# One fp32r trunk of two layers on one core: residual, second products and outputs moved from feature-major to token-major

## The reference, cut to what matters

```python
for i in range(DEPTH):                       # DEPTH = 2
    sh_m, sc_m, gt_m, sh_f, sc_f, gt_f = split(silu(c) @ ada_w[i] + ada_b[i], 6)
    h = rms_norm(x, norm_g[i, 0]) * (1.0 + sc_m) + sh_m
    y = pool_mixer(h, pool_w, pool_scale) if i == 0 else short_conv_mixer(h, conv_in_w, conv_w, conv_out_w)
    x = x + gt_m * rms_norm(y, norm_g[i, 1])
    hf = rms_norm(x, norm_g[i, 2]) * (1.0 + sc_f) + sh_f
    x = x + gt_f * rms_norm(square(relu(hf @ w1[i])) @ w2[i], norm_g[i, 3])
```

## Time and profile before

| what | value |
|---|---|
| median of three runs | 1056.64 us |
| span of the profiled execution | 1051.8 us (no other time is listed for that execution) |
| TensorE busy | 1017.9 us, 97% |
| VectorE busy | 587.5 us, 56% |
| ScalarE busy | 376.3 us, 36% |
| GpSimd busy | 43.6 us, 4% |
| mean granted TensorE clock | 0.975 |
| DMA | 140.02 MB, mean 133 GB/s |

### The profile page before, as it was taken

One profiled execution on the slowest core, in us unless ns is written; L12 is line 12 of the kernel. 1 busy time (PEld: TensorE's weight loads), 2 busy tenths in 40 slices (PEclk: granted clock), 3 DMA queues, 4 the chain that ended last, 5 costly groups with the idle time before them and its releaser, 6 DMA issues.

```text
span 1051.8 us, 11746 instructions
## 1 busy us (share of the span) xinstructions
PE 1017.9 (97%) x4594; PEld 827.0 (79%) x4594; DVE 587.5 (56%) x666; ACT 376.3 (36%) x441; POOL 43.6 (4%) x54
## 2 busy tenths in 40 slices
PE   5879899999999999998999999999999999999998
PEld 5534688888888888887888888878888888888887
DVE  4685867547547637888544444685324433432644
ACT  5364443223115223373432325355114222411533
POOL 4001410000000000001000000110000000000000
PEclk9899799999999999998999999799999999999999
DMA  7966165544555555620323223113232322223212
GB/s 264 319 213 208 41 231 205 176 166 174 208 179 180 192 187 199 221 81 1 120 81 120 80 96 104 41 46 115 87 113 80 119 80 99 100 81 118 80 40 81
DMA packets 63349, 140.02 MB, mean 133 GB/s; under 512 B 3212, under 2 KB 12628, under 8 KB 63316
## 3 DMA queue, kind: packets, MB, share of 16 engines
q1 hardware_dynamic: 55252, 110.21, 31.5%
q10 hardware_dynamic: 8064, 29.36, 7.6%
HBM read 137.47 MB, written 2.10 MB: 133 GB/s over the span
## 4 chain that ended last, share of the span: by engine, by line
PE 90%; DVE 5%; DMA 4%; ACT 1%; issue 0%; SPq 0%; DVEq 0%
PE ps L362 27%; PE ps L363 27%; PE ps L364 27%; PE ps L431 2%; DMA raw<-in_ada_w_dram 2%; PE ps L422 2%; PE ps L398 1%; DMA ada_raw<-in_ada_w_dram 1%; DVE in_lo L921 1%; DVE ada_sum L819 1%; DMA raw<-in_x_dram 1%; DVE y L932 1%; DVE xs L926 1%; DVE y L917 1%; DVE xx_t L898 1%; PE ps L415 1%
## 5 line engine op out<-in xcount | busy, mean ns | idle before, releaser
L811 DVE TENSOR_TENSOR w_lo<-raw,w_hi 128x2048 fp32r<-128x2048 f32 x77 | 176.5, 2292 | 288.0 <-ACT w_hi L604 288.0
L604 ACT ACTIVATE w_hi<-raw 128x2048 fp32r<-128x2048 f32 x81 | 154.9, 1913 | 437.7 <-PE ps L364 408.8
L362 PE MATMUL ps<-in_hi,w_hi 128*128 128x512 f32 x704 | 275.2, 391 | 7.7 <-DVE in_lo L921 6.2
L363 PE MATMUL ps<-in_lo,w_hi 128*128 128x512 f32 x704 | 274.6, 390 | 0.0
L364 PE MATMUL ps<-in_hi,w_lo 128*128 128x512 f32 x704 | 274.4, 390 | 0.0
L362 PE MATMUL ps<-mid_hi,w_hi 128*128 128x512 f32 x576 | 224.2, 389 | 0.0
L364 PE MATMUL ps<-mid_hi,w_lo 128*128 128x512 f32 x576 | 224.1, 389 | 0.0
L363 PE MATMUL ps<-mid_lo,w_hi 128*128 128x512 f32 x576 | 224.1, 389 | 0.0
L362 PEld LDWEIGHTS ps<-in_hi,w_hi 128*128 128x128 f32 x704 | 132.6, 188 | 36.7 <-issue 4.8
L364 PEld LDWEIGHTS ps<-in_hi,w_lo 128*128 128x128 f32 x704 | 132.6, 188 | 27.6
L363 PEld LDWEIGHTS ps<-in_lo,w_hi 128*128 128x128 f32 x704 | 132.6, 188 | 27.4
(11 more groups left out here) (123 smaller groups left out, 659.5 us busy)
## 6 DMA issues: line engine op xcount, KB each, us to landing
raw<-in_ffn_w_dram SPq DMA_DIRECT2D x64, 1024.0 KB, 5.3
ada_raw<-in_ada_w_dram ACTq DMA_DIRECT2D x56, 512.0 KB, 5.6
ada_raw<-in_ada_w_dram SPq DMA_DIRECT2D x28, 512.0 KB, 5.2
raw<-in_conv_in_w_dram SPq DMA_DIRECT2D x16, 512.0 KB, 4.3
raw<-in_ada_w_dram SPq DMA_DIRECT2D x10, 512.0 KB, 6.8
raw<-in_conv_in_w_dram SPq DMA_DIRECT2D x4, 1024.0 KB, 5.1
raw<-in_conv_out_w_dram SPq DMA_DIRECT2D x4, 1024.0 KB, 5.0
raw<-in_x_dram SPq DMA_DIRECT2D x4, 512.0 KB, 5.2
```

What stands on the lines that cost most here:

```text
L362: nc.tensor.matmul(o, a, hi[:, chunks[kk], :], start=first and kk == 0, stop=False)
L363: nc.tensor.matmul(o, a, lo[:, chunks[kk], :], start=False, stop=False)
L604: nc.scalar.activation(w_hi[:, u % 2, :], raw[:, u % 2, :], ACT.Copy).then_inc(w_hi_ready, 1)
L811: nc.vector.tensor_tensor(w_lo[:, u % 2, :], raw[:, u % 2, :], w_hi[:, u % 2, :].bitcast(F32), ALU.subtract).then_inc(w_lo_ready, 1)
```

## The change

- xs and y hold 128 tokens on the partitions and 1024 channels along them (four token tiles). The second product of each MLP, the convolution's output product and the pool's product take the activations (mid_hi, mid_lo, in_hi, in_lo) as stationary operand and 512 (pool: 256) columns of weights as moving one, so that their output is token-major. First products stay as they were.
- The mean square is a ScalarE Square with accumulation along a tile, one root and one reciprocal per partition. Diagonals, sums over partitions by ones and `keep_warm` are gone.
- A boundary goes by token tile: y is finished, x made, scaled by a row (128 copies of 1+scale times g), shifted by a row, turned by eight transposes into two PSUM banks, rounded by ScalarE, and the low part made by VectorE. The last pair of units goes tile by tile and the first pair of the next sub-layer in two halves of 256 tokens.
- The gate, scale and shift rows of the first sub-layers are spread by TensorE (`spread_row`, `shift_unit`), the seven later ones by GpSimd (a sum over all partitions), which also fetches the norm weights, spreads them, clears the sums and loads biases into them.
- Split weights have three slots. VectorE makes the low part of all units. The 56 later multiply-adds of ada rows are spread over layer 0's MLP (24), the convolution (24) and layer 1's MLP (8), and SyncE loads for them. All loops are unrolled.
- The output needs no turning.

```diff
-RAW_SLOTS = 2
+RAW_SLOTS, W_SLOTS = 2, 3
...
+ADA_DVE = 4 * NC
...
+SLOTS = tuple(i % 5 if i < 28 else (i - 28) % 3 for i in range(ADA_FIRST + 8 * len(LATER_SEGS)))
...
-        xs = sb("xs", [P, NC, T])
+        xs = sb("xs", [P, NT, D])
...
+            for i in range(2 * NC):
+                load_ada(i)
+            load(POOL_U)
+            for i in range(2 * NC, ADA_FIRST - 4):
+                load_ada(i)
+            load(1)
+            for i in range(ADA_FIRST - 4, ADA_FIRST):
+                load_ada(i)
+            load(2)
+            for u in range(3, UNITS):
+                load(u)
...
+            def tok_products(u, k, t, p, chunk, start, stop):
+                s = u % W_SLOTS
+                return three(bank(p, t), mid_hi[:, chunk, toks(t)], mid_lo[:, chunk, toks(t)],
+                             w_hi[:, s, k * UN:(k + 1) * UN], w_lo[:, s, k * UN:(k + 1) * UN], start, stop)
...
+            def first_pair(b, u, p, free, between, cols=COLS):
+                for side in (0, 1):
+                    tokens = toks(2 * side, 2)
+                    pe.wait_ge(h_lo, b * NT + 2 * side + 2)
+                    for kk in (0, 1):
+                        need_weights(u + kk)
...
+                        if side == 0:
+                            between(kk)          # turns token tile 2 + kk
...
+            def last_tok_pair(b, u, p, free):
+                need_weights(u)
+                need_weights(u + 1)
+                for t in range(NT):
+                    free(t)
+                    for k in range(2 * UK):
+                        if b < 3 and (t, k) == (2, 5):
+                            turn_tokens(b, 0)
+                        if b < 3 and (t, k) == (3, 6):
+                            turn_tokens(b, 1)
...
+            for t in range(NT):
+                pool_tile(t)                     # 24 products of 256 columns
+                if t >= 2:
+                    shift_unit(t - 2)            # waits for ada load 32 + t - 2; two fp32 products
+            spread_row(1, 4 * NC, 4)
+            for k in range(2, NC):
+                shift_unit(k)
+            turn_tokens(0, 0)
+            turn_tokens(0, 1)
```

ScalarE and VectorE at the pool and at boundaries 1 and 2:

```diff
+            for t in range(NT):                  # ScalarE, pool
+                y_squares(0, 0, t)
+                y_root(0, t)
+                x_root(0, t)
+            split_hi(1)
+            split_hi(2)
+            split_hi(3)
+            act.wait_ge(ada_rows, NC)
+            nc.scalar.activation(sh_row[:, :].rearrange("p (a n) -> p a n", a=2), ps[:, 6:8, :], ACT.Copy).then_inc(sh_ready, 1)
...
+            for t in range(NT):                  # VectorE, pool
+                add_ada(3 * NC + 2 * t)
+                make_v(0, 0, t)
+                add_ada(3 * NC + 2 * t + 1)
+                new_x(0, t)
+            split_lo(1)
...
+                split_hi(u)                      # ScalarE, boundary
+                for t in range(NT):
+                    y_first(b, t)
+                y_squares(b, 1, 0)
+                y_root(b, 0)
+                x_root(b, 0)
+                y_squares(b, 1, 1)
+                y_root(b, 1)
+                tokens_hi(b, 0)
+                x_root(b, 1)
...
+                split_lo(u)                      # VectorE, boundary
+                if b == 1:
+                    for t in range(NT):
+                        make_v(b, 0, t)
+                finish_y(b, 0)
+                new_x(b, 0)
+                scale_h(b, 0)
+                shift_h(b, 0)
+                finish_y(b, 1)
+                tokens_lo(b, 0)
+                new_x(b, 1)
+                scale_h(b, 1)
+                shift_h(b, 1)
+                finish_y(b, 2)
+                tokens_lo(b, 1)
...
+                finish_y(b, 3)
+                split_lo(u + 1)
+                tokens_lo(b, 2)
...
+            def sum_row(s):                      # GpSimd
...
+                nc.gpsimd.partition_all_reduce(to[:, :], ada_sum[:, s % 2, :], channels=P, reduce_op=bass.bass_isa.ReduceOp.add).then_inc(row_summed, 1)
...
+            ROWS_AT = {16: 0, 24: 1, 41: 3, 45: 4, 64: 6}   # VectorE takes the row before unit w's work
```

More of the change, by code:

```diff
@@ L55 @@
+SHIFT_ROWS = {1: 3, 2: 6}
 ADA_SLOTS = 3
[L56 to L70 removed]
@@ L341, in _ @@
+            for t in range(NT):
+                for h in range(2):
+                    sp.wait_ge(x_new, 3 * NT + 2 * t + h + 1)
+                    sp.dma_start(out[0, toks(t), half(h)], xs[:, t, half(h)]).then_inc(out_done, 16)
             sp.wait_ge(out_done, 16 * 2 * NT)
@@ new lines, in hidden @@
+            def hidden(layer, q, k):
+                p = FFN_P[layer] + q * 4 + k
+                for m in range(4):
+                    n = 4 * k + m
+                    i = hid(layer, q, n)
+                    act.wait_ge(bank_done, done_value(p, m))
+                    wait_pos(act, hid_lo, i - 1)
+                    nc.scalar.activation(work[:, n % 2, :], bank(p, m), ACT.Relu).then_inc(relu_done, 1)
+                    act.wait_ge(relu_done, i + 1)
+                    nc.scalar.activation(mid_hi[:, n, :], work[:, n % 2, :], ACT.Square).then_inc(hid_hi, 1)
@@ new lines, in ffn @@
+            def ffn(layer):
+                u0, b = FFN_U[layer], 2 * layer + 1
+                for q in range(QUARTERS):
+                    for j in range(Q_UNITS):
+                        u = u0 + q * Q_UNITS + j
+                        if q == QUARTERS - 1 and j >= 6:
+                            break
+                        if u > u0:
+                            split_hi(u + 2)
+                        if j in (1, 3):
+                            hidden(layer, q, j // 2)
+                for t in range(NT):
+                    y_squares(b, 0, t)
@@ new lines, in hidden @@
+            def hidden(layer, q, k):
+                for m in range(4):
+                    n = 4 * k + m
+                    i = hid(layer, q, n)
+                    dve.wait_ge(hid_hi, i + 1)
+                    nc.vector.tensor_tensor(work[:, n % 2, :], work[:, n % 2, :], work[:, n % 2, :], ALU.mult).then_inc(hid_sq, 1)
+                    dve.wait_ge(hid_sq, i + 1)
+                    nc.vector.tensor_tensor(mid_lo[:, n, :], work[:, n % 2, :], mid_hi[:, n, :].bitcast(F32), ALU.subtract).then_inc(hid_lo, 1)
@@ new lines, in ffn @@
+            def ffn(layer):
+                for q in range(QUARTERS):
+                    for j in range(Q_UNITS):
+                        if q == QUARTERS - 1 and j >= 6:
+                            break
+                        step(FFN_U[layer] + q * Q_UNITS + j)
+                        if j in (1, 3):
+                            hidden(layer, q, j // 2)
+                        if j in (5, 7):
+                            for t in range(NT):
+                                add_y(layer, q, j // 2 - 2, t)
@@ new lines, in _ @@
+            step(OUT_U)
+            step(OUT_U + 1)
+            for t in range(NT):
+                make_v(2, 0, t)
+            boundary(2)
+            ffn(1)
+            for t in range(NT):
+                make_v(3, 0, t)
+            for t in range(NT):
+                finish_y(3, t)
+                y_recip(3, t)
+                for h in range(2):
+                    nc.vector.scalar_tensor_tensor(out=xs[:, t, half(h)], in0=y_tok[:, t, half(h)], scalar=stat(3, t, 4), in1=xs[:, t, half(h)],
+                                                   op0=ALU.mult, op1=ALU.add).then_inc(x_new, 1)
```

1376 lines of the change are left out of this document (640 added, 736 removed).

## The result

The changed kernel takes 1088.59 us (median of 4 runs, 1085.43 to 1089.97), the kernel before 1057.1 beside it: ratio 1.0311, 95% interval 1.0279 to 1.0344. It is 3% slower, where I had forecast 0.8% (1065 us), and it lies 2.6 us above my range. The profiled span is 1083.7 us, 31.9 more than the earlier trace rows; the median lies 4.9 above it. The profile is of the fastest of the four runs (1085.43 us): 1.7 of the 4.9 us lie between span and run, the rest is spread between runs, so that the 4.84 which I had added fits again is chance.

What follows compares the result with a forecast made beforehand. TensorE bounds the three long stages, so only start, boundaries and end can change. 145.3 + 348.2 + 22.4 + 174.1 + 14.8 + 348.2 + 7.0 = 1060.0, plus 4.84 from span to run: 1065 us, 0.8% slower; range 1040 to 1086.

Steps and rivals of the forecast that it cites:

- Packed stages: Two MLPs and the convolution: 3840 products at 226.7 ns, 870.5 us, unchanged; unrolling gains nothing; 256-column products take 120 ns.
- Start: Everything before the packed MLP: first product at 138.2 us, as if packed from 145.3 against 120.4 before, 24.9 lost.
- Up to the second vector nothing changes but the slots: First step of the start: only loads in flight change, five instead of seven; second vector put at 43.5 us.
- rows late: Rival, convolution and boundary 2: GpSimd sum and spread over 44 us stall TensorE; at 60 us, 1110 us; chance 0.09.
- shift product 0 ahead of pool tile 3: Start: TensorE holds this product, waiting for load 32 (95.0 us), before pool tile 3, which is done at 101.5.
- Boundaries: Losses between long stages: boundary 1 22.4 us against 23.3 before, boundary 2 14.8 against 24.4.
- The same without the additions ... the second half at 45.9: Boundary 2: boundary 1's steps without additions, second half ready 45.9 us after the last pair's start; 14.8 us lost.
- 8 us a tile: Boundary 2: VectorE's time per token tile, against 9.3 us at boundary 1.
- End: From the last tile's product to the kernel's end: 7.0 us against 13.1 before.
- The clock: Rival: TensorE's short work keeps the clock up, sparing 8.6 us of slow clock; 1056 us, no change; chance 0.20.
- Narrow products: Rival: products of 256 columns take 170 ns instead of 120, costing 34 us; about 1090 us; chance 0.05.
- Hand-offs hidden: Rival, boundaries and pool: VectorE does not stand still for the root (1.7 us a tile); 1051 or 1040 us; chance 0.24.

Runs made afterwards that it cites:

- ends_act: The changed kernel with the 26 one-column scalings of the pooling windows' edge tables on ScalarE instead of GpSimd: 1074.26 us, ratio 1.0189 to the kernel before.
- m_outer: The changed kernel with the first unit's products in a first pair's first half going bank by bank: 1078.01 us, ratio 1.0220 to the kernel before.
- all1: The changed kernel with edge tables on ScalarE, bank-by-bank first half, low part between new x and scale, shift products last: 1049.67 us, ratio 0.9951 to before.
- before_lib: The kernel before with one GpSimd spread of a spare tile added as its last work: 1063.37 us, ratio 1.0087 to the kernel before.

## Why the prediction was wrong

- **Packed stages, right.** A product of the new form costs 226.7 ns, unrolling gives nothing, and a product of 256 columns starts 0.120 us behind the last, as these of the pool's first tile show:

```profile
83.85 0.28 PE L315 MATMUL ps<-w_hi,in_lo 128*128 128x256 f32 x1
83.97 0.28 PE L313 MATMUL ps<-w_hi,in_hi 128*128 128x256 f32 x1
84.09 0.28 PE L314 MATMUL ps<-w_lo,in_hi 128*128 128x256 f32 x1
```

- **Start, wrong by 14.4 us.** The step that failed is "Up to the second vector nothing changes but the slots". It is a stretch in which I read no row of GpSimd's: before, its 26 ops ended at 14.1 and the first window product came at 17.88, so all that they slip beyond 3.7 us lies on the path. They now end at 34.7, 20.6 later, and the product comes at 34.85, 17.0 later. I priced GpSimd's new instructions where they stand (rows late, VectorE held) and not by what they do to the head of its queue. ends_act shows 13 of the 14.4 us. The later steps were right in kind and within 3 us: 24.0 for 24.8, shift product 0 ahead of pool tile 3 (24.4 us behind the pool's input, forecast 26.7), first product 150.26 - 58.04 = 92.2 us behind the second vector where I had 94.7. The first pair took 31.2 us where I had 28.9.
- **Boundaries, wrong by 2.3 and 7.7 us.** The failed step is "The same without the additions ... the second half at 45.9": it counts when VectorE has the two tiles, and leaves out that TensorE's first pair needs the last pair's banks, so that turns, which stand behind its products, come late. It was the question the prediction should have asked of each new wait: what is queued behind it. At boundary 1 everything that was counted is in the trace (9.5 for 9.3 us a tile, the root's 1.54). m_outer gives back 5.1 and 5.2 us. At boundary 2 that leaves 17.3 against my 14.8, and a second step is wrong there, "8 us a tile": it puts the wait for the turn and the rounding of the tile before at nothing, and the trace has 3.09 and 1.65 us of it and 10.6 and 9.1 a tile. m_outer leaves these waits, and no run separates what they cost of the 2.5. At boundary 1 19.6 is left against 22.4, so there two errors had nearly cancelled: in m_outer the last two tiles are ready at 51.4 (forecast 53.0), and the pair ends 11.7 us behind them, where I had 11.5 and 1.5 of slow clock.
- **End, right.** 6.3 for 7.0 us.
- **Rivals.** The clock did not hold (granted clock 0.82 at the start, 0.92 and 0.90 about the boundaries). Rows were not late: a GpSimd sum takes 6.1 us and a spread 1.3 to 3.0, against a bound of 44. Narrow products were not dear. "Hand-offs hidden" did not happen but was one edit away. The sign was right for the reason given: without GpSimd's 13 us (ends_act) the kernel is still 1.9% slower than before, and its start 26.3 us longer (forecast 24.9).

## What to carry to other kernels

Before moving work to an engine, look at what that engine does first and who waits for it: here one new kind of instruction, even as GpSimd's last, cost 7 us at the head of the queue, and the delay pushed small ops into another engine's work, which tripled their time. When a last stage and the next one's first share PSUM banks, fill them one after the other, and fill every wait for a root with the low part of the tile before (from the kernel after to all1 the boundaries lose 7.1 and 13.3 us less). A change of layout that costs the packed stages nothing is decided in the start and the hand-offs, so sum those by their orders first.

## What the runs showed that I had not expected

- Custom instructions (sum over partitions, spread) in the program: 6.9 to 7.7 us of idle GpSimd ahead of its first masked op, and another 9.45 us ahead of the first custom one (5.83 in ends_act, 7.84 in before_lib). The Trainium skill (GPSIMD Engine Reference, Instruction dispatch) tells of some 6 us for the first call to freshly loaded code, with no instruction to be seen. The second gap is of that order; the first, ahead of an ordinary op, is not what the page describes.
- One-column GpSimd ops take on average 0.23 us beside an idle VectorE and 0.68 beside a busy one, mostly with multiply-adds; the same 26 take 0.10 each on ScalarE.
- A GpSimd sum holds VectorE too. Timelines in the convolution, after, GpSimd and then VectorE:

```profile
573.82 6.11 POOL L1132 PARTITION_ALL_REDUCE gate_row<-ada_sum  x1 [139.28 <-DVE ada_sum L786]
```

```profile
575.11 3.78 DVE L1016 SCALAR_TENSOR_TENSOR y<-cu,vec,y 128x512 f32<-128x512 f32 x1 [0.79 <-ACT y L750]
578.92 0.75 DVE L1019 SCALAR_TENSOR_TENSOR y<-cu,vec,y 128x512 f32<-128x512 f32 x1
```

The op takes 3.78 us instead of 0.75, and two more of the seven sums meet an op with two SBUF inputs (3.79 and 3.89 us). It is held for 3.0 us and ends at 578.89, before the sum does (579.93): less than the sums' whole length, which the prediction had named as what would come onto VectorE. It was hidden here, as the window of 130.60 us shows; by these rows, on a busy VectorE each sum would cost some 3 us, an estimate.
